# A transformer block with product-key experts and a second block with routed experts: new order of the opening, products on constants, eight expert slots, projection ahead of the norm

## The chip, the cores and the metric

The kernel is one program on 1 core of one Trainium2 chip. The metric is the device time of one execution in microseconds (us), here the median of the runs shown. Engines: TensorE (PE; its weight loads are listed as PEld), VectorE (DVE), ScalarE (ACT), GpSimd (POOL), and SyncE (SP), which only issues transfers here.

## What is computed

All arithmetic is float32, on 256 tokens of 1024 features. The kernel works on transposed activations: features on the 128 partitions, K = 8 chunks of features, T = 256 tokens along the free dimension (TT = 2 groups of 128).

```python
# first block
mod = silu(c) @ w_mod + b_mod                       # six vectors; the same for c_ctx
h  = rms_norm(x) * (1 + sc1) + sh1                  # and hc from ctx
u  = h @ w_in                                       # queries, keys/values, conv input, gates
x  = x + g1 * merge(attention, conformer_conv, gates) @ w_out
h2 = rms_norm(x) * (1 + sc2) + sh2
x  = x + g2 * peer_ffn(h2)                          # 128 x 128 product-key experts, top 16, 8 heads
x  = rms_norm(x, final_g)
# second block
h  = rms_norm(x, ln1_g_2);  proj = h @ w_in_2       # q, k, v, then the other columns
x  = x + (sigmoid(gate) * branches) @ w_out_2       # stick-breaking attention, gated linear scan
t  = rms_norm(x, ln2_g_2)
group = argmax(t @ w_rg + b_rg); two best of the 4 experts of that group
x  = x + sum over the experts chosen: combine * (silu(t @ w_gate) * (t @ w_up)) @ w_down
return rms_norm(x, final_g_2)
```

## The kernel before, in words

There is one instruction stream per engine, written by hand, with semaphores between them. `tile_plan` numbers every PSUM tile in the order in which TensorE fills it, with the engine that reads it; tile n uses bank n % 4 of `psD`, and TensorE waits until the reader of tile n - 4 has freed it. `psY` holds four further banks, which `aux(i)` gives out. The weights come in blocks of 2 MB (128 partitions x 4096 float32) through a ring of three slots (`load`, L410); SP issues block n only when TensorE has begun with the last products on block n - 3 (`w_used`).

A float32 product stands in the trace as two MATMUL instructions, an fp32r product as one. Where fp32r is used (the first block's experts), a float32 operand is split into a rounded part and the rest (hi and lo), and both are multiplied.

**Opening (L1063 to L1103, L1496 to L1509).** ACT's queue issues cT, cst, vec, xT, ctxT and conv_w, while SP issues the first w_mod blocks. TensorE: two `modulation` blocks (L558), the sum of squares of x (`stat`, L522), `modulation_sums`, the sum of squares of ctx, two more `modulation` blocks, their sums; then the projection `u0` (pairs of 128-column groups on w_in, L522), which needs the normed hT from DVE (L1509). POOL makes the normed context (L1418, L1422) from the second root on.

**w_pq.** After the first residual, `stat_x("x1")` (L544), then DVE's inverse (L1486, L1488), ACT's root and DVE's norm (L1641, L1644), then `pair` on w_pq.

**Start of the second block (L829 to L845, L1825 to L1851).** The result of the first block's experts is turned back (L832), DVE adds it to x in eight steps (L1830), `stat_x("x2")` follows, DVE scales x by final_g and the root (`normed(7)`, L1636), `stat_x("xb")` follows on that, and `normed(8)` gives hT. Only then TensorE projects q and k (`qks`, four pairs on w_in_2), which ACT copies out.

**Routed experts.** `stat_x("x3")`, the norm, the router product (L522, 128x20), eight-chunk transposes of h into token rows (`hrow`, L953), a chain of small DVE operations (L1981 to L2065) with two exponentials on ACT, the `place` products on the mask, and then seats: each expert has 64 seats per round, `hot` says which token sits where. The 16 experts are worked in pairs. One turn of the loop does one pair, in this order on TensorE: `gate_up` of both experts (L977), `seat_tokens(0)` for the next pair (L522), transposes of hid (L1016), `seat_tokens(1)`, `down` of the first (L987), two transposes of the weighted `hot` (L1026), `down` of the second, and the scatter to tokens (L1035), which adds yrow x hotT to psY in float32. ACT makes the silu and copies one half of yrow and the seated rows, DVE multiplies (L2087) and copies the other half (L2090, L2094).

```python
        mslot = [ring[(STREAM["moe"] + i) % RING] for i in range(3)] + [ar(20480 + SLOT * i, SLOT) for i in range(3)]
        ...
            used = (2, 2, 4, 4, 5, 6)
            ...
            with sp.Fori(1, turns) as n:
                for j in range(6):
                    sp.wait_ge(m_used, n * 6 + (used[j] - 6))
                    expert_load(j, ...)
```

A turn needs six blocks of 2 MB (gate, up of two experts, then two down); there are six slots, and a slot is asked for again in the turn after. Three of the first six blocks are loaded when the ring is free, three after `x_ready` reaches 32 (L479).

## Time and profile before

| | |
|---|---|
| median of 3 runs | 1931.45 us (1930.93 to 1932.64) |
| profiled execution | 1933.67 us, its span 1931.8 us |
| TensorE matmul busy | 1798.2 us (93%) |
| DVE / ACT / POOL busy | 1018.2 / 615.1 / 161.3 us |
| mean granted TensorE clock | 0.967 |
| bytes | 343.45 MB, 178 GB/s over the span |

The span runs from the first to the last instruction; the execution takes 1.9 us more than it. A line of a timeline has: start in us, length in us, engine, line of the kernel, operation, what it writes and reads, its shape, the number of instructions merged into it, and in brackets the idle time of the engine before it and what ended that. In the table of stretches each engine has its busy time and number of instructions; then come the granted TensorE clock (1.00 is full speed), the busy share of the DMA engines, and GB/s.

### The profile page before, as it was taken

The page shows a single profiled execution, that of the slowest core. Times are in us where ns is not written, and L with a number is a line of the kernel's source. Part 1 is how long each engine was busy: PE and PEld are TensorE (multiplying, and loading weights), DVE is VectorE, ACT ScalarE, POOL GpSimd, SP SyncE. Part 2 cuts the span into 40 slices and gives each one's busy share as a digit, 9 for nine tenths or more (in the row PEclk, how much of TensorE's full clock was granted, in tenths as well). Part 3 has the DMA queues.
Part 4 walks back from the last instruction along what each step waited for, and adds up shares of the span by engine and source line. Part 5 has one row for each costly group of instructions (what it writes and reads, how often), then busy time and mean ns, then how long its engine had stood idle before and what let it go on. Part 6 is the DMA issues. An engine that isn't in the chain of part 4 may idle for free. (4 is left out here: it accounts for less than half of the span.)

```text
span 1931.8 us, 23571 instructions
## 1 busy us (share of the span) xinstructions
PE 1798.2 (93%) x8906; PEld 1389.8 (72%) x8906; DVE 1018.2 (53%) x2015; ACT 615.1 (32%) x875; POOL 161.3 (8%) x81
## 2 busy tenths in 40 slices
PE   4999989999998999899999999997997989799997
PEld 2877646778887998677888888886776867544443
DVE  2469755220898876777767767765025432211112
ACT  2111264101111665333454554553353120111111
POOL 1200000000001996100000000000000000000000
PEclk8999999999999999999999999999998989799999
DMA  6466321233442222455555555555331315499993
GB/s 279 177 253 236 134 87 44 93 126 128 160 178 78 88 88 103 159 194 186 180 182 193 185 185 195 180 189 199 131 131 48 127 46 211 175 399 403 419 403 141
DMA packets 33325, 343.45 MB, mean 178 GB/s; under 512 B 3952, under 2 KB 4464, under 8 KB 5104
## 3 DMA queue, kind: packets, MB, share of 16 engines
q1 hardware_dynamic: 31680, 338.70, 46.1%
q10 hardware_dynamic: 1584, 3.90, 0.5%
q8 instruction: 42, 0.69, 0.1%
q14 instruction: 19, 0.16, 0.0%
HBM read 340.49 MB, written 2.10 MB: 177 GB/s over the span
## 5 line engine op out<-in xcount | busy, mean ns | idle before, releaser
L522 PE MATMUL psD<-xh,ring 128*128 128x256 f32 x1984 | 442.1, 384 | 18.9 <-DVE arena L1949 5.3
L522 PEld LDWEIGHTS psD<-xh,ring 128*128 128x128 f32 x1984 | 379.3, 192 | 79.4 <-issue 20.7
L797 PE MATMUL psY<-ring_r,work_r 128*128 128x512 f32 x1536 | 370.5, 396 | 11.2 <-DVE ring_r L1761 11.2
L1053 ACT ACTIVATE arena<-psD 128x512 f32<-128x512 f32 (+5 forms) x211 | 146.3, 701 | 708.9 <-PE psD L522 491.9
L797 PEld LDWEIGHTS psY<-ring_r,work_r 128*128 128x128 f32 x1536 | 283.0, 190 | 80.7 <-issue 17.8
L1053 ACT ACTIVATE ring_r<-ring 128x1024 fp32r<-128x1024 f32 x196 | 200.2, 1055 | 167.6 <-PE psY L797 113.1
L783 PE MATMUL psD<-xh_r,ring_r 128*128 128x512 f32 x544 | 194.1, 397 | 0.0
L1761 DVE TENSOR_TENSOR ring_r<-ring,ring_r 128x1024 fp32r<-128x1024 f32 x128 | 160.7, 1255 | 15.1 <-ACT ring_r L1053 15.0
L522 PE MATMUL psD<-arena,ring 128*128 128x256 f32 (+1 forms) x640 | 150.5, 395 | 7.4 <-DVE arena L1964 4.1
L785 PE MATMUL psD<-xh_r,ring_r 128*128 128x256 f32 x544 | 152.6, 280 | 0.0
L522 PEld LDWEIGHTS psD<-arena,ring 128*128 128x128 f32 (+1 forms) x640 | 119.5, 189 | 37.3 <-issue 8.8
L783 PEld LDWEIGHTS psD<-xh_r,ring_r 128*128 128x128 f32 x544 | 102.2, 188 | 24.5
L977 PE MATMUL psD<-ring,arena 128*64 128x512 f32 x384 | 111.5, 594 | 0.9 <-ACT arena L1053 0.9
L785 PEld LDWEIGHTS psD<-xh_r,ring_r 128*128 128x128 f32 x544 | 102.6, 189 | 2.6
L1436 POOL TENSOR_TENSOR ring<-cst,pick 128x384 f32<-128x384 f32 x32 | 59.2, 1849 | 538.3 <-PEq L745 536.7
L1756 DVE TENSOR_TENSOR ring_r<-ring,ring_r 128x1024 fp32r<-128x1024 f32 x68 | 83.3, 1225 | 37.7 <-ACT ring_r L1053 37.7
L522 PE MATMUL psD<-arena 128*128 128x128 f32 (+4 forms) x388 | 81.4, 354 | 15.9 <-DVEq L2036 6.9
L756 PE MATMUL psY<-xh,ring 128*128 128x256 f32 x384 | 90.7, 387 | 3.0 <-DVE pick L1712 3.0
L1535 DVE SCALAR_TENSOR_TENSOR arena<-arena,pick 128x256 f32<-128x256 f32 x232 | 92.5, 480 | 0.0
L977 PEld LDWEIGHTS psD<-ring,arena 128*64 128x64 f32 x384 | 35.6, 137 | 71.1 <-issue 71.1
L756 PEld LDWEIGHTS psY<-xh,ring 128*128 128x128 f32 x384 | 72.2, 195 | 12.1 <-issue 3.2
L2087 DVE TENSOR_TENSOR arena<-arena,psD 64x512 f32<-64x512 f32 x16 | 11.0, 690 | 130.4 <-ACT arena L1053 130.4
(238 smaller groups left out, 1906.4 us busy)
## 6 DMA issues: line engine op xcount, KB each, us to landing
ring<-in_tables SPq DMA_DIRECT2D x68, 1024.0 KB, 4.8
ring<-in_experts SPq DMA_DIRECT2D x24, 2048.0 KB, 9.2
arena<-in_experts SPq DMA_DIRECT2D x24, 2048.0 KB, 14.7
ring<-in_w_in SPq DMA_DIRECT2D x20, 2048.0 KB, 8.3
ring<-in_early_v SPq DMA_DIRECT2D x30, 1024.0 KB, 4.8
ring<-in_w_mod SPq DMA_DIRECT2D x12, 2048.0 KB, 8.4
ring<-in_early_u SPq DMA_DIRECT2D x9, 2048.0 KB, 8.5
ring<-in_mid_u SPq DMA_DIRECT2D x12, 1024.0 KB, 4.8
```

What stands on the lines that cost most here:

```text
L522: last = nc.tensor.matmul(dst, a, b, start=(i == 0), stop=(i == len(pairs) - 1))
L756: last = nc.tensor.matmul(psY[:, 1024 + 512 * (m % 2) + j * T:1024 + 512 * (m % 2) + (j + 1) * T], col_slot[m % 3][:, at:at + P], hT[:, k, ...
L783: nc.tensor.matmul(bank[:, :], u_hi[c % 2][:, k * P:(k + 1) * P], xh_r[:, :, k, :], start=(k == 0), stop=(k == K - 1), skip_group_check=True)
L785: last = nc.tensor.matmul(bank[:, 0:T], lo[:, k * P:(k + 1) * P], h_hi[:, k, :], start=False, stop=(k == K - 1), skip_group_check=True)
L797: last = nc.tensor.matmul(psY[:, t * D + h * 512:t * D + (h + 1) * 512], wgt[:, b, t * P:(t + 1) * P], v[:, h * 512:(h + 1) * 512], start= ...
L977: last = nc.tensor.matmul(psD[bank][lo:lo + 64, :], lhs, wt[:, k * 512:(k + 1) * 512], start=(k == 0), stop=(k == K - 1))
L1053: return nc.scalar.activation(dst, src, f, **kw)
L1436: nc.gpsimd.tensor_tensor(one_b[:, h, DVE_B:], iota8[:, 0:8 - DVE_B], e2.broadcast_to([P, 8 - DVE_B, P]), ALU.subtract).then_inc(b_diff, 1)
L1535: s[j % 2] = mark(stt(acc, y[:, j:j + T], conv_w[:, m * TAPS + j:m * TAPS + j + 1], acc, ALU.mult, ALU.add))
L1756: tt(col_lo[unit][:, 0:D], col_slot[unit][:, 0:D], u_hi[c % 2].bitcast(F32), ALU.subtract).then_inc(u_lo_ready, 1)
L1761: tt(lo, a, v_hi[b].bitcast(F32), ALU.subtract).then_inc(v_lo_ready, 1)
L2087: tt(hid[64 * side:64 * (side + 1), :], sgl[64:128, side, :], psD[bank][64:128, :], ALU.mult).then_inc(hid_done, 1)
```

## The change

1. Opening: SP's queue issues cT, cst, xT and vec ahead of the w_mod blocks; ACT's queue keeps ctxT and conv_w. TensorE takes the sum of squares of x before the modulation, and that of ctx between blocks 2 and 3. The modulation blocks get the order shown. POOL waits for hT before it norms the context.
2. `keep(n, bank)`: n float32 products of the identity with 512 columns of constants, in a bank that nobody reads. There are 27 of them: 8 in the opening, 3 after `stat_x("x1")`, 3 after `stat_x("x3")`, 7 after the transposes of h, 6 before the first `seat_tokens`.
3. Second block: DVE makes `xg` = x * final_g * ln1_g beside the residual. The projection `qks` runs on xg, the two sums of squares (of x, and of x * final_g, squared by ACT) come after its first pair, and DVE multiplies q and k by the common root while it copies them out. hT comes from the same root.
4. Routed experts: seats and scatter use fp32r on split operands (hrow, yrow in hi and lo parts); the combine weight goes into hid instead of `hot` (a product with `seat_col`, copied to `seat_scale`). The scatter of a turn runs in the next turn, after its first `gate_up`. Four turns are written out, the loop goes over fours. `place` leaves the tile plan and uses psY.
5. Eight slots for the expert blocks, free when `gate_up` or `down` is done; the second w_out2 block goes to a place of its own in the arena, and the first expert blocks are issued from `osb_ready` on.

```diff
+            sp.dma_start(cT[:].rearrange("p a b -> p (a b)"), w["cT"]).then_inc(in_c, 16)
+            sp.dma_start(cst[:], w["cst"]).then_inc(in_small, 16)
+            sp.dma_start(xT[:].rearrange("p a b -> p (a b)"), w["xT"]).then_inc(in_x, 16)
+            sp.dma_start(vec[:], w["vec"]).then_inc(in_small, 16)
             for i in range(4):
                 load(STREAM["mod1"] + i, w["w_mod"][i])
...
-            act.dma_start(cT[:].rearrange("p a b -> p (a b)"), w["cT"]).then_inc(in_c, 16)
-            act.dma_start(cst[:], w["cst"]).then_inc(in_small, 16)
-            act.dma_start(vec[:], w["vec"]).then_inc(in_small, 16)
-            act.dma_start(xT[:].rearrange("p a b -> p (a b)"), w["xT"]).then_inc(in_x, 16)
...
+            def keep(n, bank):
+                for _ in range(n):
+                    nc.tensor.matmul(bank, ident, cst[:, 0:512], start=True, stop=True)
+
+            pe.wait_ge(in_small, 32)
+            keep(2, psD[3])
+            pe.wait_ge(sq_ready, 1)
+            stat("x", ones, chunks(sq))
             pe.wait_ge(c_silu, 1)
             pe.wait_ge(mparts_zero, 1)
             for b in range(2):
                 modulation(b, STREAM["mod1"] + b, b)
-            pe.wait_ge(in_small, 32)
-            pe.wait_ge(sq_ready, 1)
-            stat("x", ones, chunks(sq))
             modulation_sums(TILE["mod1_"], 0)
+            keep(2, psD[3])
+            modulation(2, STREAM["mod1"] + 2, 1)
             pe.wait_ge(sq_ready, 2)
             stat("ctx", ones, chunks(csq))
-            for b in range(2, 4):
-                modulation(b, STREAM["mod1"] + b, 1)
+            keep(2, psD[3])
+            modulation(3, STREAM["mod1"] + 3, 1)
             modulation_sums(TILE["mod1_"] + 1, 2)
+            keep(2, psD[3])
...
             pool.wait_ge(rstd_ready, 2)
+            pool.wait_ge(h_ready, K)
...
             stat_x("x1", sq, 0)
+            keep(3, aux(2))
...
-            stat_x("x2", sq2, 1)
-            stat_x("xb", sq2, 2)
             for m in range(4):
                 wt = use(STREAM["w_in2"] + m // 2)
-                pair(TILE["qks"] + m, wt, 2 * (m % 2), hT, 1 if m == 2 else 0, None if m else (h_part, K))
+                pe.wait_ge(xg_ready, 2)
+                pair(TILE["qks"] + m, wt, 2 * (m % 2), xg, 1 if m == 2 else 0, None if m else (xg_ready, 0))
+                if m == 0:
+                    stat_x("x2", sq2, 1)
+                    stat_x("xb", sq2g, 2)
...
+            r = rstd(8)
+            for k in range(K):
+                stt(hT[:, k, :], xT[:, k, :], both_g[:, k:k + 1], r, ALU.mult, ALU.mult).then_inc(h_part, 1)
+            for m in range(4):
+                ps = take(TILE["qks"] + m).rearrange("p (a t) -> p a t", a=2)
+                dst = (qs if m < 2 else ks)[:, 2 * (m % 2):2 * (m % 2) + 2, :]
+                stt(dst, ps, SBD ** -0.5 if m < 2 else 1.0, over(r, 2), ALU.mult, ALU.mult).then_inc(tile_free["dve"], 1)
...
-            stat_x("x3", sq2, 3, frees=1)
+            stat_x("x3", sq2, 3)
+            keep(3, aux(3))
...
+            keep(7, aux(3))
             pe.wait_ge(mask_ready, 1)
...
+            def turn(it, t, after):
+                def slot(j):
+                    b = 6 * t + j
+                    pe.wait_ge(m_loaded[b % 8], it * 48 + (16 * (b // 8) + 16))
+                    return mslot[b % 8]
+
+                pe.wait_ge(seated_ready, it * 8 + (2 * t + 2))
+                if after:
+                    pe.wait_ge(yrow_ready, it * 16 + (4 * t - 2))
+                gate_up(1, 0, slot(0), slot(1))
+                if after:
+                    pe.wait_ge(yrow_ready, it * 16 + 4 * t)
+                    scatter()
+                turn_seats()
+                gate_up(3, 1, slot(2), slot(3))
+                pe.wait_ge(hot_ready, it * 4 + (t + 2))
+                pe.wait_ge(hotT_ready, it * 4 + (t + 1))
+                seat_tokens(0)
+                pe.wait_ge(hid_done, it * 8 + (2 * t + 2))
+                for f in range(4):
+                    last = nc.tensor.transpose(psD[2][:, f * P:(f + 1) * P], hid[:, f * P:(f + 1) * P], ident)
+                last.then_inc(hidT_done, 1)
+                pe.wait_ge(seated_ready, it * 8 + (2 * t + 3))
+                seat_tokens(1)
+                pe.wait_ge(hidT_ready, it * 4 + (t + 1))
+                down(1, 0, slot(4))
+                down(3, 1, slot(5))
+
+            pe.wait_ge(hrow_ready, 4)
+            keep(6, psD[1])
             pe.wait_ge(rounds_ready, 1)
...
+            def scatter():
+                for m in range(K):
+                    for rows in (yrow_hi, yrow_lo):
+                        last = nc.tensor.matmul(psY[:, m * T:(m + 1) * T], rows[:, m * P:(m + 1) * P], hotT,
+                                                start=False, stop=False, skip_group_check=True)
+                last.then_inc(scattered, 1)
...
+            def slot_free(b, it=0):
+                n, j = divmod(b - 8, 6)
+                done = gu_done if j < 4 else down_done
+                sp.wait_ge(done, it * 8 + (2 * n + (1 if j in (0, 1, 4) else 2)))
...
+            for n in range(4):
+                ps = psD[(TILE["hrow"] + n) % 4]
+                dve.wait_ge(hrow_hi_ready, n + 1)
+                at = slice((n % 2) * 512, (n % 2 + 1) * 512)
+                tt(hrow_lo[:, n // 2, at], ps, hrow_hi[:, n // 2, at].bitcast(F32), ALU.subtract).then_inc(hrow_ready, 1)
             dve.wait_ge(rexp, 2)
```

## Rows read from the trace of the kernel before

**Rows 1.** Page, part 1: busy time of TensorE over the span

```profile
PE 1798.2 (93%) x8906; PEld 1389.8 (72%) x8906; DVE 1018.2 (53%) x2015; ACT 615.1 (32%) x875; POOL 161.3 (8%) x81
```

**Rows 2.** Stretches: busy PE, PEld, DVE, ACT, POOL, then clock, DMA share, GB/s

```profile
9.50:29.00 19.50, 6.01 (x32) 0.74 (x32) 0.00 (x0) 2.25 (x3) 0.00 (x0) 0.66 0.98 413
44.00:49.50 5.50, 1.46 (x14) 1.37 (x13) 4.08 (x6) 0.43 (x2) 4.98 (x2) 0.73 1.00 429
...
419.00:424.00 5.00, 4.83 (x12) 3.87 (x13) 4.24 (x14) 0.00 (x0) 0.00 (x0) 0.50 0.54 170
...
1335.70:1341.60 5.90, 5.87 (x16) 4.49 (x16) 1.12 (x3) 2.90 (x4) 0.00 (x0) 0.62 0.99 418
...
1637.80:1644.40 6.60, 6.54 (x31) 6.57 (x32) 2.69 (x7) 0.00 (x0) 0.00 (x0) 0.50 1.02 434
...
1662.00:1666.90 4.90, 3.75 (x16) 3.49 (x16) 0.58 (x2) 0.59 (x1) 0.00 (x0) 0.50 0.00 0
...
1733.06:1763.78 30.72, 29.58 (x151) 13.90 (x151) 4.05 (x7) 5.32 (x8) 0.00 (x0) 1.00 0.97 405
```

**Rows 3.** DMA issues: KB, us to landing (x; first w_in_2 block, issued 1323.3)

```profile
xh<-in_xT ACTq DMA_DIRECT2D x1, 1024.0 KB, 25.2
...
ring<-in_w_in SPq DMA_DIRECT2D x1, 2048.0 KB, 8.0
```

**Rows 4.** Timeline of the opening

```profile
29.42 5.37 PE L522 MATMUL psY<-arena,cst 128*128 128x256 f32 x16 [11.79 <-ACT arena L1053]
...
42.81 5.96 POOL L1418 TENSOR_TENSOR arena<-arena,work 128x2048 f32<-128x2048 f32 x1 [42.36 <-ACT work L1053]
...
45.78 3.04 DVE L1503 TENSOR_TENSOR mod<-mod,vec 128x32 f32<-128x32 f32 x1 [1.35 <-ACT mod L1053]
...
49.30 4.77 POOL L1422 TENSOR_SCALAR arena<-arena,gx,mod 128x256 f32<-128x256 f32 x8 [0.52 <-DVE gx L1506]
...
49.70 15.84 PE L522 MATMUL psD<-xh,ring 128*128 128x256 f32 x64 [4.24 <-DVE xh L1509]
```

**Rows 5.** Timeline, first products on w_pq

```profile
419.17 20.99 PE L522 MATMUL psD<-xh,ring 128*128 128x256 f32 x82 [4.09 <-DVE xh L1644]
```

**Rows 6.** Timeline, start of the second block

```profile
1325.38 3.23 DVE L1830 SCALAR_TENSOR_TENSOR xh<-psD,mod,xh 128x256 f32<-128x256 f32 x8 [0.82 <-PE psD L832]
...
1345.02 27.86 PE L522 MATMUL psD<-xh,ring 128*128 128x256 f32 x128 [3.42 <-DVE xh L1636]
```

**Rows 7.** Timeline from the router to the first turn

```profile
1637.86 6.99 PE L522 MATMUL psD<-arena,xh 128*128 128x20 f32 x32 [3.36 <-DVE xh L1636]
...
1650.15 0.16 DVE L2010 TENSOR_REDUCE arena<-arena 128x2 f32<-128x8 f32 x1 [3.58 <-ACT arena L1053]
...
1659.65 0.42 DVE L2074 TENSOR_TENSOR arena<-cst,arena 128x256 f32<-128x256 f32 x1
...
1662.52 3.75 PE L522 MATMUL psD<-arena 128*128 128x128 f32 x16 [5.43 <-DVE psY L2075]
...
1671.61 7.48 PE L977 MATMUL psD<-ring,arena 128*64 128x512 f32 x33 [0.88 <-ACT arena L1053]
```

**Rows 8.** Timeline, one turn of the expert loop

```profile
1733.06 7.51 PE L977 MATMUL psD<-ring,arena 128*64 128x512 f32 x33
...
1760.16 3.69 PE L1035 MATMUL psY<-arena 128*128 128x256 f32 x16 [0.89 <-DVE arena L2094]
```

**Rows 9.** Timeline, rows that serve as prices

```profile
34.63 1.84 PE L522 MATMUL psD<-cst,arena 128*128 128x2 f32 x16
...
1303.62 0.28 PE L785 MATMUL psD<-xh_r,ring_r 128*128 128x256 f32 x1
1303.73 0.40 PE L783 MATMUL psD<-xh_r,ring_r 128*128 128x512 f32 x1
...
1423.43 7.13 PE L522 MATMUL psD<-ring,xh 128*128 128x512 f32 x16
...
1583.01 0.69 DVE L1612 TENSOR_TENSOR arena<-psD,arena 128x512 f32<-128x512 f32 x1 [3.66 <-PE psD L522]
```

More of the change, by code:

```diff
@@ L495, in _ @@
+            fours = sp.value_load(rounds[0:1, 1:2], min_val=PAIRS // 4, max_val=PAIRS // 4 * ROUNDS)
+            with sp.Fori(1, fours) as it:
+                for b in range(24):
+                    slot_free(b, it)
+                    expert_load(b, w["experts"][bass.ds(it % (PAIRS // 4) * 24 + b, 1)].rearrange("a p n -> (a p) n"))
             for half in range(2):
@@ L967, in seat_tokens, with gate_up @@
                     last = group(psD[0][:, j * P:(j + 1) * P],
-                                 [(hrow[:, t, k * P:(k + 1) * P], hot[:, t, :]) for t in range(TT)])
+                                 [(rows[:, t, k * P:(k + 1) * P], hot[:, t, :])
+                                  for t in range(TT) for rows in (hrow_hi, hrow_lo)])
                 last.then_inc(seated_done, 1)
-            def gate_up(bank, side, wg, wu, frees):
+            def gate_up(bank, side, wg, wu):
                 for k in range(K):
@@ L2095, in _ @@
+            dve.wait_ge(yrow_ready, turns * 4)
+            dve.sem_inc(yrow_all, 1)
             dve.wait_ge(scattered, turns)
```

275 lines of the change are left out of this document (145 added, 130 removed).

## The prediction

> **What bounds the kernel now.** I read the page first, then the list of what TensorE waited for, then the table of stretches with the granted clock, and last the timelines of the places that the change touches. TensorE is busy 93% of the span [rows 1], so a gain can only come from its idle gaps, from stretches at the lower clock, or from products taken off it. The change touches five places, and each has one of these. In the opening TensorE waits 11.79 us for the square of x [rows 4], and x had landed only 25.2 us after its issue [rows 3], while the w_mod blocks filled the DMA engines at 413 GB/s [rows 2]. Around each norm it idles 3 to 5 us and then works for some us at clock 0.50, the lower of its two levels (1.2 GHz): on w_pq, on the second sum of squares, on the router and on the first seats [rows 2]. In the expert loop a turn takes 30.72 us at clock 1.00 [rows 2], the eight turns fill 1671.61 [rows 7] to 1917.4, and no row shows TensorE waiting for a load; but the DMA engines are at 0.97 and 405 GB/s there, and the highest rate elsewhere is 429 to 434 [rows 2], so the loop is near both bounds.
>
> **Opening.** All bytes ahead of x in its queue are now cT and cst (0.33 MB); beside it runs ctxT (1.05 MB) from the other queue. 0.33 + 1.05 + 1.05 = 2.4 MB at 430 GB/s are 5.7 us, from a start at about 2.2 us: x lands near 8.5 us instead of 27.4, vec near 9, the three first w_mod blocks (4.9 us each) near 13.7, 18.6 and 23.4. Then, with my estimates between the prices of the rows (a sum of squares is 3.6 us at full clock and 5.4 as it ran here [rows 4]; a group of sums 1.84 [rows 9]): two constant products and the sum of x to 18; modulation 0 and 1 to 22 (block 3 is issued at about 19 and lands at 28.3); copies and sums to 24.5, constants to 26, modulation 2 to 28 (its first product issues w_in, which lands near 33 behind block 3), the sum for ctx to 32, constants, modulation 3 to 35.5, copy and sums to 38. Before, DVE's small addition to mod took 3.04 us, exactly until POOL's 5.96 us operation was over [rows 4]; POOL now waits for hT, so it takes 0.2. hT starts near 39 and TensorE near 39.8 instead of 49.70. The 64 products took 15.84 us, partly at the lower clock; full clock is 64 x 0.217 = 13.9 (27.86 / 128 = 0.217 [rows 6]), 1.5 less counting what the ramp leaves. POOL's context (5.96 + 4.77 us [rows 4]) starts at about 42 and ends at 53, just as these products end. What follows is bound by TensorE as before, so this is a clean shift: **-11.4 us**. Bounds: -7, if all of it runs at the lower clock and the constants are not covered; -14, if full clock holds from the start.
>
> **w_pq.** A constant product is two instructions of 512 columns, 2 x 0.43 = 0.86 us (16 took 7.13 [rows 9]); three are 2.6 us inside a gap of 4.09 [rows 5], so they cost nothing; their cover is DVE's and ACT's norm, without it they would cost 2.6. The first 5.0 us after the gap ran at 0.50 [rows 2], so up to half of it comes back: **-2.6 us**. Bounds 0 (clock falls all the same) and -2.8.
>
> **Second block.** DVE's residual takes 3.23 us for eight steps [rows 6]; xg adds a step of some 0.25 us to each, all done by about 1331. The first products could start at 1327, but what is late next is w_in_2: its first block, issued at 1323.3, lands 8.0 us later [rows 3], at 1331.3. From there: one pair 6.95 (27.86 / 4 [rows 6]), two sums 7.2, three pairs 20.9, and 2.5 us for a cold start, since TensorE idles 4.7 us before and there is no constant product here; the same idle time before the second sum gave 5.87 us for 16 instructions at mean clock 0.62 [rows 2]. End at 1368.9, before 1345.02 + 27.86 = 1372.9. **-4.0 us**; bounds -6.5 (no cold start) and -1 (ACT's eight extra squares or DVE late). DVE's root is ready near 1352 and hT near 1355, ahead of the next user of hT at 1369. DVE's later norm of x (3.3 us) and its four copies of q and k (0.69 each [rows 9]) run beside 14 us of products on v.
>
> **Router to first turn.** The three constants (2.6 us) fill a gap of 3.36 [rows 7]. The router's 32 instructions took 6.99 us at 0.50; at full clock 16 of them follow DVE's norm and the others take 0.115 each (1.84 / 16 [rows 9]), the logits come 2.1 us earlier. DVE's 3.58 us wait before 1650.15 is for an exponential behind ACT's copies of hrow [rows 7]; copies and table load move with the transposes, so that end comes 2.8 us earlier. Seven constants take 6.0 us, from about 1644.5 to 1650.5, the mask is due at 1651.9. DVE's four subtractions for hrow_lo cost 4 x 0.69 = 2.8 us [rows 9] and stand on its path, with 0.4 for two small additions and 0.3 back from the place products. So hot is ready about when it was, 1660.1. TensorE began its seats at 1662.52, held by the clearing of psY [rows 7], which the first scatter now waits for instead. Six constants from 1654.9 end at 1660.0, just in time; with the register load I take 1661.0: -1.5. The seats: 2 x 3.75 us at 0.50 [rows 2, 7] become 2 x 1.85: -3.8. **-5.3 us**; bounds 0 and -8.
>
> Here one price is open: an fp32r product of 128 columns with new weights. Products of 256 columns follow each other in 0.11 us (1303.62 to 1303.73), and 16 float32 instructions with only two columns still take 1.84 us, 0.115 each [rows 9]. I take 0.115 for 128 columns too, since that row is the one in which the load of 128x128 weights decides; then splitting in hi and lo leaves a seat group as long as it was (16 instructions, 1.8 us). The other end is 0.058, half of the 256-column row. The Trainium skill, TensorE: Matmul & The Clock Gate, section LDWEIGHTS (loading the stationary operand), speaks against a gain from this part: it puts a weight load at columns divided by 1.2 GHz whatever else is streamed, 107 ns for 128. By that page's figure, as an estimate, a seat group would be 1.7 us, by the column count 0.9; the two-column row agrees with the page.
>
> **Loop.** Per turn: the scatter was 3.62 us (16 float32 instructions, from 1760.16 to the next gate_up, one turn of 30.72 after 1733.06 [rows 8]), now 16 fp32r at 0.115: -1.8. Its wait of 0.89 us for DVE [rows 8] goes, as the next gate_up stands ahead of it: -0.9. Four small products of two instructions each, with 64-column weights, at most 8 x 0.115: I take +0.5. Seats 0. So 28.5 us; bounds 27.3 (seats at the other price; the first seat group must still cover ACT's silu and DVE's product) and 29.8. DVE's four subtractions and ACT's four copies per turn (2.8 and 2.4 us) run beside `down` and `gate_up`; their cover is 20 us. Loads: six blocks of 2.1 MB in 28.5 us would be 441 GB/s, above 434. But eight are there before the first turn, so 40 are left, the first issued 7 us into turn 0 and the last needed 24 us into turn 7: 217 us for 84 MB, 387 GB/s. At 405 GB/s they take 207 us. So the slots bridge it, and loads don't bind by 10 us. Eight turns are 228 us. The last scatter waits for two ACT copies and a subtraction, 2.2 us instead of 0.9. 230.2 us against 245.9: **-15.7 us**, bounds -26 and -6.
>
> **Sum.** 11.4 + 2.6 + 4.0 + 5.3 + 15.7 = 39.0 us. The profiled execution took 1933.67 us, so 1894.7 on its scale; the median of the runs is 2.2 us below, so **1892.5 us**. A measurement of this kernel tells about 0.2% (3.9 us) from no change.
>
> **Rivals.**
> *The constants don't hold the clock.* For: they come after gaps, and the stretch 9.5 to 29 had 0.66 with 6 us of products in it [rows 2]. Against: the constants leave 1.5 us of the 4.09 on w_pq, and the loop, with gaps of 0.9 us in it, stands at 1.00 [rows 2, 8]. If they don't, each constant costs 1.72 us. Opening -6; w_pq 5.2 us into a gap of 4.1: +1.1; second block -4; three constants overrun by 1.8, seven end near 1661.5 instead of the mask at 1654.8, six more 10.3 us, seats at the old price: first turn near 1683, +11.5; loop -15.7. About -13: **1918 us**. Chance 0.09.
> *Loads bind in the loop.* For: 0.97 busy at 405 GB/s already [rows 2]. It decides below 387 GB/s. If the rate is 370, 40 loads take 227 us, and the loop lasts 7 + 227 + 3.6 for the last `down` + 4.1 to the end of the scatter = 242 us, a gain of 4 instead of 15.7: **1904 us**. Chance 0.09.
> *The opening is bound by w_in and w_mod, not by x.* Before w_in can be used, 12.4 MB must land, and w_in is only issued when block 2 is in use. If interleaving with ctx holds w_mod back by one block (5 us), the gain there is 6: **1898 us**. Chance 0.08.
> *The other side: loads one at a time.* SP now waits for each slot in order; if each load begins only when the one before has landed, it costs 8.0 us [rows 3], and 40 take 320 us: the loop lasts some 335 us, +89, less the 23.3 elsewhere: **1997 us**. It decides from 30.7 + 23.3 / 8 = 33.6 us per turn, 374 GB/s from start to end. Against: before, SP waited in the same way and reached 405. Chance 0.03.
> *The change does less than it says*, as the fours are rounded up and idle turns are run: no, before there were eight turns, which is two fours. Not priced.
>
> **Numbers.** My forecast, all five parts within their bounds, has 0.71. Its own range is 1880 to 1905: the bounds of the parts don't all fall on one side. The upper end goes to 1910 to take in the two rivals at 1898 and 1904 with their own spread; left out are the first rival, the last, and a part of the low end. Faster by over 0.2%: 0.95; within 0.2%: 0.01; slower: 0.04.
>
> **What the profile after would show.** x lands within 10 us; u0 starts at 38 to 42 with clock 1.00; DVE's addition to mod takes 0.2 us. The first products on w_pq, the router and the seats stand at clock 1.00. The first pair of the second block starts at 1320 (1331.3 less the shifts so far), released by the load of w_in_2. Turns 28.5 us apart, no wait for a load; a seat group of 1.8 us. The forecast is wrong if a load releases gate_up or down, if TensorE's constants are the last thing ahead of w_pq or of the first seats, or if turns stay above 30 us.

## The result, and the profile after

The changed kernel takes **1898.64 us** (median of 4 runs, 1895.24 to 1900.81), the kernel before beside it 1931.36 us (1930.93 to 1932.64): ratio 0.9828, 95% interval 0.9811 to 0.9845. The profiled execution took 1899.66 us, with a span of 1897.6, against 1933.67 and 1931.8. The forecast of 1892.5 was 6.1 us too low, and the measured time lies inside its range of 1880 to 1910; the profiled executions are 34.0 us apart, not 39.0.

First the page of the kernel after, part 1, for TensorE [rows 1], then its table of stretches, columns as in [rows 2]:

```profile
PE 1806.9 (95%) x9024; PEld 1404.1 (74%) x9024; DVE 1031.9 (54%) x2060; ACT 623.3 (33%) x891; POOL 159.4 (8%) x81
```

```profile
251.90:256.90 5.00, 4.97 (x12) 2.86 (x13) 2.60 (x8) 2.67 (x8) 0.00 (x0) 0.50 0.73 246
407.40:412.40 5.00, 5.00 (x17) 2.79 (x18) 4.05 (x13) 0.00 (x0) 0.00 (x0) 1.00 0.71 229
1317.80:1327.60 9.80, 9.80 (x33) 8.21 (x34) 0.00 (x0) 4.00 (x8) 0.00 (x0) 0.72 0.98 418
1638.20:1643.00 4.80, 4.76 (x11) 2.20 (x12) 4.00 (x29) 0.00 (x0) 0.00 (x0) 1.00 0.86 355
...
1646.00:1648.20 2.20, 2.12 (x16) 2.12 (x16) 0.00 (x0) 0.03 (x1) 0.00 (x0) 0.84 0.00 0
1649.10:1658.70 9.60, 9.53 (x32) 2.74 (x32) 0.00 (x0) 1.30 (x2) 0.00 (x0) 0.73 0.00 0
1700.00:1728.30 28.30, 28.07 (x162) 15.23 (x160) 5.36 (x10) 6.52 (x11) 0.00 (x0) 1.00 1.00 426
...
1883.10:1888.50 5.40, 5.32 (x16) 4.14 (x16) 1.22 (x4) 3.10 (x4) 0.00 (x0) 0.69 0.00 0
```

TensorE is at full clock on w_pq, where it was at 0.50 [rows 2], and in the constants ahead of the seats. Its clock falls again in places that the forecast had at full clock: the second seat group (1646), the first `gate_up` behind it (1649.1, 9.6 us for what takes 7.0 in later turns) and the last sum of squares (1883.1). The turn is 28.3 us instead of 30.72. Below, "cold" means at the lower clock.

Timeline of the opening, after; it answers to [rows 4]:

```profile
9.55 1.91 ACT L1122 ACTIVATE arena<-xh 128x2048 f32<-128x2048 f32 x1 [4.76 <-DMA xh<-in_xT]
9.75 3.78 PE L620 MATMUL psD<-cst 128*128 128x512 f32 x4 [9.75 <-DMA vec<-in_vec]
...
13.32 4.92 PE L554 MATMUL psY<-arena,cst 128*128 128x256 f32 x16
...
37.03 0.19 DVE L1567 TENSOR_TENSOR mod<-mod,vec 128x32 f32<-128x32 f32 x1 [3.37 <-ACT mod L1122]
...
38.44 13.98 PE L554 MATMUL psD<-xh,ring 128*128 128x256 f32 x64
...
40.36 4.51 POOL L1481 TENSOR_TENSOR arena<-arena,work 128x2048 f32<-128x2048 f32 x1 [39.91 <-DVE xh L1573]
```

x is there at 9.5 instead of 27.4, DVE's addition takes 0.19 instead of 3.04 us, and the 64 products of u0 take 13.98 instead of 15.84 and begin 11.3 earlier. The first four constant instructions take about 0.9 us each, twice the 0.43 of later ones, so they are cold, although the granted clock of 9.70 to 13.30 reads 1.00: at the start of this kernel the lengths show the lower clock and that column doesn't.

Timeline of the later places, after; they answer to [rows 5], [rows 6] and [rows 7]; the last three rows are the end of the loop:

```profile
407.38 5.00 PE L554 MATMUL psD<-xh,ring 128*128 128x256 f32 x16 [1.51 <-DVE xh L1708]
...
1317.80 9.84 PE L554 MATMUL psD<-arena,ring 128*128 128x256 f32 x32 [4.76 <-DMA ring<-in_w_in]
...
1619.69 5.60 PE L554 MATMUL psD<-arena,xh 128*128 128x20 f32 x32 [0.79 <-DVE xh L1700]
...
1638.24 5.42 PE L620 MATMUL psD<-cst 128*128 128x512 f32 x12 [1.36 <-DVE hrow_lo L2131]
...
1878.59 0.39 PE L1056 MATMUL psY<-hotT,yrow_hi 128*128 128x256 f32 x1 [2.19 <-DVEq L2190]
...
1881.58 2.74 DVE L2193 TENSOR_TENSOR xh<-psY,xh 128x256 f32<-128x256 f32 x8 [3.10 <-PE psY L1056]
...
1883.14 5.32 PE L576 MATMUL psY<-arena,cst 128*128 128x256 f32 x16 [1.60 <-ACT arena L1122]
```

The same events in both traces give the account of the gain:

| part | event | before | after | gain | forecast |
|---|---|---|---|---|---|
| opening | end of u0's 64 products | 65.37 | 52.25 | 13.1 | 11.4 |
| (nothing changed) | attention, at L698 (before L657) | 292.39 | 280.60 | -1.3 | 0 |
| w_pq | first tile copied out | 429.41 | 415.87 | 1.75 | 2.6 |
| second block | first products on v | 1372.72 | 1355.11 | 4.1 | 4.0 |
| its middle | sum of squares x3 | 1630.88 | 1612.71 | 0.6 | 0 |
| router to first turn | first `gate_up` | 1671.61 | 1649.17 | 4.3 | 5.3 |
| loop, last scatter | DVE's last addition begins | 1917.50 | 1881.58 | 13.5 | 15.7 |
| last sum and norm | last norm begins | 1925.54 | 1891.27 | -1.7 | 0 |

Together 34.3 us. Where the gain fell short, TensorE's clock was low in most rows; so the experiments ask two things, what each part is worth by itself, and what the clock follows.

### The profile page after: what moved, and what is told of

Same layout as the page of the kernel before. It is cut to its first block and busy times, and to the rows that moved or that the text cites. A ratio compares the mean times of both kernels' runs of the same rounds, so it can differ in the third digit from the quotient of the medians.

```text
span 1897.6 us, 23793 instructions
## 1 busy us (share of the span) xinstructions
PE 1806.9 (95%) x9024; PEld 1404.1 (74%) x9024; DVE 1031.9 (54%) x2060; ACT 623.3 (33%) x891; POOL 159.4 (8%) x81
## 5 line engine op out<-in xcount | busy, mean ns | idle before, releaser
L554 PE MATMUL psD<-xh,ring 128*128 128x256 f32 x1856 | 411.0, 382 | 8.9 <-DVE arena L2037 5.6
L554 PEld LDWEIGHTS psD<-xh,ring 128*128 128x128 f32 x1856 | 351.5, 191 | 67.0 <-issue 15.4
L1122 ACT ACTIVATE arena<-psD 128x512 f32<-128x512 f32 (+4 forms) x187 | 132.2, 715 | 616.1 <-PE psD L554 473.2
L554 PE MATMUL psD<-arena,ring 128*128 128x256 f32 x704 | 167.6, 398 | 12.2 <-DMA ring<-in_w_in 4.8
L554 PEld LDWEIGHTS psD<-arena,ring 128*128 128x128 f32 x704 | 133.6, 192 | 44.7 <-issue 8.8
L1028 PE MATMUL psD<-arena 128*64 128x512 f32 x320 | 115.8, 602 | 0.7 <-ACT arena L1122 0.7
L1028 PE MATMUL psD<-ring,arena 128*64 128x512 f32 x192 | 87.2, 608 | 0.0
L1503 POOL TENSOR_TENSOR work<-work,pick 128x1024 f32<-128x1024 f32 x32 | 79.1, 2473 | 0.0
```

The costliest lines, as they stand in the source:

```text
L554: last = nc.tensor.matmul(dst, a, b, start=(i == 0), stop=(i == len(pairs) - 1))
L1028: last = nc.tensor.matmul(psD[bank][lo:lo + 64, :], lhs, wt[:, k * 512:(k + 1) * 512], start=(k == 0), stop=(k == K - 1))
L1122: return nc.scalar.activation(dst, src, f, **kw)
L1503: nc.gpsimd.tensor_tensor(one_a[:, h], one_a[:, h], g.broadcast_to([P, 8, P]), ALU.mult).then_inc(a_ready, 1)
```

## The experiments

Each median stands beside 1898.64 us for the changed kernel. Runs of one and the same kernel lie up to 8 us apart here, so where a difference is small, the traces decide and not the medians.

**No constants.** `keep` does nothing:

```diff
-                for _ in range(n):
-                    nc.tensor.matmul(bank, ident, cst[:, 0:512], start=True, stop=True)
+                return
```

> The changed kernel with all 26 constant products left out (eight in the opening, three ahead of w_pq, three ahead of the router, twelve ahead of the first seats). Theory (they hold the clock where TensorE would idle): w_pq starts where it did but at the lower clock for about 5 us, +1.8; the router at the lower clock, logits 2 us later; both seat groups at the lower clock, 3.7 us each, so the first gate_up comes 2 to 4 us later than now. In the opening about 9 us of constants leave TensorE's path, but sums and modulations then run partly at the lower clock: between -4 and +2. Together +1 to +8, 1900 to 1907 us. Rival (the clock falls or stays whatever they do, as it fell in the second seat group right behind six of them): the time falls by what they occupy, the opening by 4 us or more and nothing elsewhere, 1891 to 1895 us.

(There are 27 constants, not 26.) Measured: 1902.11 us (1897.32 to 1905.57), +3.5, inside the theory's 1900 to 1907; the ratio 0.9843 [0.982, 0.9867] overlaps that of the changed kernel. The timeline without constants, opening and router:

```profile
37.78 15.74 PE L554 MATMUL psD<-xh,ring 128*128 128x256 f32 x64 [1.32 <-DVE xh L1572]
...
1621.87 6.86 PE L554 MATMUL psD<-arena,xh 128*128 128x20 f32 x32 [3.37 <-DVE xh L1699]
```

u0 starts 0.7 us earlier, but at the lower clock, and ends 1.1 later. The router takes 6.86 instead of 5.60, and from the sum x3 to the first seats it is 31.5 instead of 30.4. The two seat groups up to the first `gate_up` take 8.7 us instead of 6.1. On w_pq the first tile is copied out 17.9 us after the sum x1 begins, instead of 16.2. So the constants hold the clock for the most part and are worth 6.5 us in these four places (1.1 + 1.7 + 1.1 + 2.6); the profiled executions are 5.7 apart. The opening's eight give only 1.1: there they cost TensorE nearly as much as they save.

**Scatter ahead of `gate_up`.** The order of the turn undone, the hi and lo products kept:

```diff
                 if after:
-                    pe.wait_ge(yrow_ready, it * 16 + (4 * t - 2))
-                gate_up(1, 0, slot(0), slot(1))
-                if after:
                     pe.wait_ge(yrow_ready, it * 16 + 4 * t)
                     scatter()
+                gate_up(1, 0, slot(0), slot(1))
```

> The changed kernel with each turn's scatter ahead of the next turn's first gate_up, waiting for both hi and lo rows, instead of behind it. Theory (the order hides the copy and subtraction behind a gate_up): the last scatter shows this wait, 2.19 us, so each of the seven other turns gets about 2.2 us longer, 30.5 instead of 28.3, and if the wait lets the clock fall as at the end of the kernel, up to 2 us more: +15 to +25, 1914 to 1924 us. Rival (the loads set the turn, and the order is worth nothing, the gain being that of eight slots): turns stay at 28.3 to 28.8, 1899 to 1903 us.

Measured: 1915.76 us (1912.87 to 1917.11), +17.1, as the theory said. The first row of the scatter in its timeline, and one turn in its table of stretches:

```profile
1709.19 0.36 PE L1056 MATMUL psY<-hotT,yrow_hi 128*128 128x256 f32 x1 [2.23 <-DVE yrow_lo L2185]
```

```profile
1700.00:1730.87 30.87, 28.42 (x160) 15.16 (x162) 5.36 (x10) 6.51 (x11) 0.00 (x0) 1.00 0.98 408
```

The wait is 2.23 us; before, with one copy instead of a copy and a subtraction, it was 0.89 [rows 8]. The turn is 30.87 us, no shorter than the 30.72 of before: **in the old order the split into hi and lo saves nothing**, since the longer way to yrow_lo takes back what the cheaper products give. Only with the scatter behind the next `gate_up` does it pay. The clock stayed at 1.00 in spite of the wait.

**Scatter in float32,** on the hi rows alone, order as changed:

```diff
-                    for rows in (yrow_hi, yrow_lo):
-                        last = nc.tensor.matmul(psY[...], rows[:, m * P:(m + 1) * P], hotT, ...)
+                    last = nc.tensor.matmul(psY[...], yrow_hi[:, m * P:(m + 1) * P].bitcast(F32), hotT.bitcast(F32), ...)
```

> The changed kernel with the scatter as eight float32 matrix products on the hi rows alone (the lo rows are still made but left out of the product, so the output lacks their part), instead of sixteen fp32r ones. Theory (a float32 product of 256 columns costs 2 x 0.217 us, an fp32r one 0.115): the scatter goes from 1.9 to 3.6 us, turns from 28.3 to 30.0, +13 to +15 in eight scatters, 1912 to 1915 us. Rival (the turn has slack behind loads or behind DVE and the shorter scatter bought little): under +5, 1904 us at most.

Measured: 1910.28 us (1908.72 to 1911.89), +11.6, a little under the 13 to 15 expected; its turn is 29.86 us, 1.56 longer, and its scatter:

```profile
1712.33 3.72 PE L1055 MATMUL psY<-hotT,yrow_hi 128*128 128x256 f32 x16
```

Eight scatters at 1.56 are 12.5. With the 0.89 of the wait this is the turn's whole gain: 30.72 - 1.56 - 0.89 = 28.27, measured 28.30. So the cheaper scatter gives 1.6 us and not the 1.8 of the forecast, and the rest of the turn, with the four small products that it put at +0.5, costs next to nothing.

**Six blocks back.** `slot_free` waits as if there were six slots:

```diff
-                n, j = divmod(b - 8, 6)
+                n, j = divmod(b - 6, 6)
```

> The changed kernel with its eight slots, but each load waits until the block six places back, not eight, has been used, which is what six slots would do. Theory (loads don't bind with eight, by some 10 us, and nearly do with six; a turn of six loads at 425 GB/s takes 29.6 us): TensorE waits for a load in each turn, the turn goes from 28.3 to 29.6 to 30.5 us, +8 to +18, 1907 to 1917 us. Rival (the loads were never near, TensorE's own work alone set the turn): no wait, 1899 us as now.

Measured: 1895.80 us (1893.81 to 1898.65), no slower; the theory expected a wait for a load in each turn, and the rival was right. One turn:

```profile
1700.00:1728.30 28.30, 28.07 (x160) 15.23 (x158) 5.36 (x10) 6.51 (x10) 0.00 (x0) 1.00 1.01 428
```

The turn is 28.30 to the hundredth, at 428 GB/s. At that rate six blocks take 29.4 us, 1.1 more than a turn, so each turn eats into the lead; but eight blocks are still loaded ahead of the first turn here, and, as an estimate, eight turns lose 8 x 1.1 = 9 us of it, the time of two blocks. A kernel that also starts with six was not tried.

This run shows something else. Up to the loop it is the changed kernel, instruction for instruction, and it reached the first silu at 1653.06, the changed kernel at 1658.85. Of these 5.8 us, 2.0 lie ahead of the attention (1.7 of them in one sum of 16 products, 3.72 us here and 5.41 in the changed kernel), 2.6 in the attention's first 28 us, 1.2 between w_pq and the end of the first block's experts. The attention's start in it, against 251.90 above:

```profile
249.90:254.90 5.00, 4.74 (x22) 2.95 (x23) 3.90 (x12) 3.88 (x11) 0.00 (x0) 1.00 0.75 249
```

From the attention's first product behind its wait of 2.22 us (251.93 in the changed kernel) to the one behind its next wait (0.87 us, 280.60) all kernels run the same products. The traces show three lengths: 26.0 us (this and `scatter_first`), 27.3 (before, `no_constants`, `scatter_f32`, `seats_f32`, `sums_first`, `ctx_late`) and 28.6 to 28.7 (the changed kernel, `no_pool_wait`, `x_first_alone`, `more_constants`). The clock falls behind that wait or it doesn't, and comes back sooner or later, from run to run. **That is the -1.3 of the table, in a part that nobody changed**, and, at up to 2.7 us, a good part of the spread between runs.

**More constants,** in five places: ahead of w_pq, of the second block's first pair, behind each of the two seat groups ahead of the loop, and on both sides of the last scatter:

```diff
-            keep(3, aux(2))
+            keep(4, aux(2))
...
+            keep(4, aux(3))
...
             seat_tokens(0)
+            keep(1, psD[1])
             pe.wait_ge(seated_ready, 1)
             seat_tokens(1)
+            keep(1, psD[1])
...
+            keep(2, psD[2])
             pe.wait_ge(yrow_all, 1)
             scatter()
+            keep(2, psD[2])
             stat_x("x4", sq2, 4)
```

> The changed kernel with constants in five more places: a fourth ahead of w_pq, four ahead of the second block's first pair (a wait of 4.8 us for w_in_2), one behind each of the two seat groups ahead of the loop, two ahead of the last scatter (2.2 us wait) and two behind it. Theory (the shortfall against the forecast is the lower clock in these places, and products that fill the wait hold it up): first pair of the second block 7.0 instead of 9.8 us, second seat group at 0.11 a product and first gate_up of turn 0 in 7.0 instead of 9.7 us at the price of up to 0.9, last scatter at 0.12 a product and the last sum of squares in 3.6 instead of 5.3. Together -5 to -9, 1890 to 1894 us. Rival (the clock doesn't follow what is put into a gap of a few us; it fell in the second seat group behind six constants): under 2 us, or up to 2 slower, 1897 to 1901 us.

Measured: 1893.24 us (1887.08 to 1894.51), -5.4. Its stretches (both seat groups, the first `gate_up`, the last scatter and sum), then its first pair:

```profile
1645.90:1647.80 1.90, 1.90 (x18) 1.88 (x17) 0.00 (x0) 0.00 (x0) 0.00 (x0) 1.00 0.00 0
1648.70:1655.70 7.00, 7.00 (x33) 2.21 (x32) 0.00 (x0) 1.16 (x1) 0.00 (x0) 1.00 0.00 0
...
1875.60:1877.60 2.00, 1.96 (x16) 1.97 (x17) 0.00 (x0) 0.00 (x0) 0.00 (x0) 1.00 0.00 0
1879.40:1883.10 3.70, 3.70 (x17) 2.94 (x16) 1.19 (x4) 3.07 (x4) 0.00 (x0) 1.00 0.00 0
```

```profile
1317.43 7.17 PE L554 MATMUL psD<-arena,ring 128*128 128x256 f32 x32 [1.40 <-DMA ring<-in_w_in]
```

Each place is at full clock and as long as the theory said: 7.0 instead of 9.7 for the first `gate_up`, 3.7 instead of 5.3 for the last sum, 7.2 instead of 9.8 for the first pair. The trace gives 2.7 in the pair, 2.8 from seats to silu and 2.4 at the end, 7.9 in all; the median and the profiled executions show 5.4 and 5.5. The difference lies between the sum x3 and the first seats, which took 32.9 us instead of 30.4, where this edit changed nothing:

```profile
1636.38 7.11 PE L620 MATMUL psD<-cst 128*128 128x512 f32 x12 [1.35 <-DVE hrow_lo L2135]
```

The same six constants that took 5.42 us in the changed kernel began cold here (0.74 over the group), took 7.11 and ran 2.0 us past `hot`, which was ready at 1640.94. So a constant costs its length once the clock is low under it, and what is held in one place can partly be lost in the next.

**Seats in float32,** on the hi rows alone:

```diff
-                                 [(rows[:, t, k * P:(k + 1) * P], hot[:, t, :])
-                                  for t in range(TT) for rows in (hrow_hi, hrow_lo)])
+                                 [(hrow_hi[:, t, k * P:(k + 1) * P].bitcast(F32), hot[:, t, :].bitcast(F32))
+                                  for t in range(TT)])
```

> The changed kernel with each seat group as 8 float32 products of 128 columns on the hi rows alone (the lo rows are made but left out of it, so the output lacks their part) instead of 16 fp32r ones. Theory of the prediction (a product of 128 columns is set by its weight load, 0.115 us an instruction in either form): a seat group stays 1.8 us at full clock, turns stay at 28.3: within 2 us of 1899. Rival (the columns decide for fp32r and it was the cheaper form): a turn longer by 1 us or more, 1907 us and up. In the same run: does the clock fall in the second seat group ahead of the loop, as with fp32r? Then it is the shape, not the form.

Measured: 1891.51 us (1890.25 to 1893.57), -7.1, outside both ranges. One turn is 28.41 us and not 28.30, so the theory's price was right: 16 instructions of 128 columns take as long in either form, 0.11 to 0.12 us each. The Trainium skill, TensorE: Matmul & The Clock Gate, section LDWEIGHTS (loading the stationary operand), puts a weight load at its columns divided by 1.2 GHz, as an estimate 107 ns for 128 columns; the trace agrees, with these 0.11 to 0.12 us. The gain is elsewhere, first in its second seat group and first `gate_up`:

```profile
1644.60:1646.70 2.10, 2.05 (x16) 1.86 (x16) 0.00 (x0) 0.00 (x0) 0.00 (x0) 1.00 0.00 0
1647.30:1654.30 7.00, 6.95 (x32) 2.21 (x32) 0.00 (x0) 1.28 (x1) 0.00 (x0) 1.00 0.00 0
```

They are at full clock, with gaps of 0.69 us around them as in the changed kernel. In the eight traces with fp32r seats and no constant between the groups, the first silu came 9.4 to 9.8 us after the first `gate_up` began; here it came after 7.1. The kernel before supports the same reading: its float32 seat groups were themselves cold (0.50), and `gate_up` behind them began at 1.00, its silu 7.1 us later [rows 7], while behind the cold fp32r groups of `no_constants` it came after 9.5. So at this place it is the form, not the shape, that goes with the fall; why is not shown.

From seats to silu that is 3.3 us. Another 2.4 lie at the end, where the last scatter, in fp32r and behind the same wait of 2.19 us, stayed at 1.00 and so did the last sum:

```profile
1878.82 3.69 PE L576 MATMUL psY<-arena,cst 128*128 128x256 f32 x16 [1.60 <-ACT arena L1122]
```

With 1.3 in the attention and 0.9 lost in eight turns that makes 6.1, as far as the profiled executions are apart.

**x first, alone:** the kernel before, its four transfers moved from ACT's queue to SP's, in the order of the change, and nothing else.

```diff
-            act.dma_start(xT[:].rearrange("p a b -> p (a b)"), w["xT"]).then_inc(in_x, 16)
...
+            sp.dma_start(xT[:].rearrange("p a b -> p (a b)"), w["xT"]).then_inc(in_x, 16)
+            sp.dma_start(vec[:], w["vec"]).then_inc(in_small, 16)
             for i in range(4):
                 load(STREAM["mod1"] + i, w["w_mod"][i])
```

> The kernel before with one edit: cT, cst, x and vec issued on SyncE's queue ahead of w_mod, as the change does; TensorE's order, no constants and the second processor's context operation as before. Theory (the late x was only half of it: TensorE waited 11.8 us for it, but then w_mod and DVE's 3.0 us addition beside GpSimd stand next): x lands by 10 us, u0 starts near 42 instead of 49.7, so -6 to -9, 1921 to 1925 us. Rival (moving x alone gives the whole opening, the reordering and constants nothing): -11 to -13, 1917 to 1920 us.

Measured: 1924.03 us (median of 6, 1919.70 to 1927.38), ratio 0.9964 [0.9947, 0.9981], -6.4. Its timeline:

```profile
36.05 3.05 DVE L1503 TENSOR_TENSOR mod<-mod,vec 128x32 f32<-128x32 f32 x1 [1.35 <-ACT mod L1057]
...
39.97 15.49 PE L526 MATMUL psD<-xh,ring 128*128 128x256 f32 x64 [4.24 <-DVE xh L1509]
```

u0 starts at 39.97 instead of 49.70, so the queue gives 9.7 of the opening's 11.3; the addition beside POOL is still 3.05 us, and the products still run at the lower clock. With 0.35 from their shorter time it is 10.1 by the end of these products, of 13.1. The median shows -6.4, inside the theory's range, and the profiled executions are 10.1 apart; so this part's worth lies between, and the rival (-11 to -13) is not borne out.

**No wait on GpSimd:**

```diff
             pool.wait_ge(rstd_ready, 2)
-            pool.wait_ge(h_ready, K)
```

> The changed kernel without GpSimd's wait for hT: its context operation may run as soon as the root is there, near 34, beside DVE's work on hT. Theory (the two share something, and GpSimd's operation stalled DVE's addition to mod for 3.0 us before): DVE's addition takes 3 us instead of 0.19, its steps for hT 0.5 instead of 0.33 each, u0 starts 3 us later, +3, 1901 to 1903 us. Rival (the addition was held by something else, or GpSimd is through before it matters): u0 at 38.4, 1899 us.

Measured: 1896.59 us (1895.57 to 1902.94), not told from 1898.64. Its timeline:

```profile
34.11 4.51 POOL L1480 TENSOR_TENSOR arena<-arena,work 128x2048 f32<-128x2048 f32 x1 [33.66 <-ACT work L1122]
...
36.95 1.72 DVE L1566 TENSOR_TENSOR mod<-mod,vec 128x32 f32<-128x32 f32 x1 [3.37 <-ACT mod L1122]
...
38.98 3.98 DVE L1572 TENSOR_SCALAR xh<-arena,gx,mod 128x256 f32<-128x256 f32 x8
39.14 4.78 POOL L1484 TENSOR_SCALAR arena<-arena,gx,mod 128x256 f32<-128x256 f32 x8 [0.52 <-DVE gx L1569]
```

DVE's addition, 0.19 us by itself, lasts until POOL's operation is over: 34.11 + 4.51 = 38.62, 36.95 + 1.72 = 38.67. The eight steps beside POOL's next ones take 3.98 instead of 2.67. u0 starts 1.1 us later and ends 1.7 later. So the stall is real, but POOL's early start leaves only its tail; the theory's 3 us was too much. The Trainium skill, SBUF — State Buffer, section "SBUF: two separate sides", says that VectorE and GpSimd share one port pair, and that when a VectorE operation with two inputs in SBUF meets a GpSimd operation that reads SBUF, the one that starts first holds the pair for its whole instruction; the two end times agree.

**Sums first,** in the second block:

```diff
+            stat_x("x2", sq2, 1)
+            stat_x("xb", sq2g, 2)
             for m in range(4):
...
-                if m == 0:
-                    stat_x("x2", sq2, 1)
-                    stat_x("xb", sq2g, 2)
```

> The changed kernel with the two sums of squares ahead of the four unscaled pairs of the second block, not behind the first of them. Theory (the gain there comes from the projection not waiting for a norm at all; the sums then fill TensorE's wait for w_in_2, but run at the lower clock behind a gap of their own): the pairs end within 2 us of now, -2 to +2, 1897 to 1901 us. Rival (the order is what gains: a pair under the squares of ScalarE): +4 or more, 1903 us and up.

Measured: 1891.17 us (1889.31 to 1895.92), -7.5, better than either expected. Its timeline:

```profile
1309.14 1.97 PE L874 MATMUL psD<-cst,arena 128*128 128x128 f32 x16 [1.38 <-DVE arena L1888]
1311.62 2.35 PE L576 MATMUL psY<-arena,cst 128*128 128x256 f32 x8 [0.51 <-ACT arena L1121]
1314.15 1.13 PE L576 MATMUL psY<-arena,cst 128*128 128x256 f32 x4 [0.18 <-ACT arena L1121]
1315.46 4.58 PE L576 MATMUL psY<-arena,cst 128*128 128x256 f32 x20 [0.18 <-ACT arena L1121]
1319.88 27.79 PE L554 MATMUL psD<-arena,ring 128*128 128x256 f32 x128
```

The sums do useful work in the wait for w_in_2, and their gaps are 0.51 us at most, so the clock never fell; the load was there when they ended. From the end of the transposes the pairs end 36.4 us later, 42.1 in the changed kernel: -5.7. I had taken a sum as 7 us *behind* a wait; it fits *into* it.

**ctx late:**

```diff
-            sp.dma_start(vec[:], w["vec"]).then_inc(in_small, 16)
+            load(STREAM["mod1"], w["w_mod"][0])
+            load(STREAM["mod1"] + 1, w["w_mod"][1])
+            sp.dma_start(ctxT.rearrange("p a t -> p (a t)"), w["ctxT"]).then_inc(in_ctx, 16)
+            sp.dma_start(vec[:], w["vec"]).then_inc(in_vec, 16)
...
-            pe.wait_ge(in_small, 32)
+            pe.wait_ge(in_small, 16)
...
-            dve.wait_ge(in_small, 32)
+            dve.wait_ge(in_small, 16)
+            dve.wait_ge(in_vec, 16)
```

> The changed kernel with the opening's transfers in another order: ctx on SyncE's queue behind the second w_mod block, vec behind it with a semaphore of its own, and TensorE's first constants waiting for cst alone. Theory (the opening is a chain on TensorE that begins with vec, at 9.75 us, and x, at 9.5; ctx is not needed before 27): x lands near 6, the sum for x starts near 9 instead of 13.3, u0 near 35 instead of 38.4: -2 to -4, 1895 to 1897 us. Rival (the opening is bound by the bytes of w_mod and w_in, the DMA engines being full to 30 us): u0 stays at 38, 1899 us.

Measured: 1900.46 us (1899.07 to 1902.02), +1.8: neither. Its timeline:

```profile
21.58 0.43 DVE L1552 TENSOR_SCALAR work<-psY 128x256 f32<-128x256 f32 x1 [19.63 <-DMA vec<-in_vec]
```

x landed at 9.03 instead of 9.55, so ctx was only 0.5 us of its delay. The w_mod blocks issued behind x in the same queue are the likely rest; no run held them back. And the late vec held DVE to 21.58, ACT's root behind it, and ACT's copy of the second modulation behind that. u0 started at 43.38.

**Together:** the edits of `sums_first` and `more_constants` (without the four ahead of the pair), and

```diff
+            keep(2, aux(2))
             pe.wait_ge(conv_ready, K)
             stat("mean", ones, chunks(convz))
...
+            keep(2, aux(2))
             for n in range(8):
                 ps = tile(TILE["v"] + n)
...
+            keep(2, aux(2))
             pe.wait_ge(q_ready, 8)
```

> The changed kernel with the sums of the second block first (as in sums_first), the constants of more_constants except those ahead of the second block's first pair, which the sums now fill, and two constants in each of three waits of 1.9 to 2.2 us that the changed kernel still has (ahead of the sum for the mean, ahead of the products for v, ahead of the attention). Theory (each place adds up on its own): -5.8 in the second block, -5.2 at seats, last scatter and last sum (as measured in more_constants), and up to 2.6 where the clock fell in the attention's start in some runs and not in others: 1885 to 1889 us, and a narrower spread between runs. Rival (the clock's dips only move: what is held in one place falls in the next): no better than either edit alone, 1891 to 1894 us.

Measured: 1885.95 us (median of 5, 1884.27 to 1887.88), as the theory said, with a narrow spread. The constants ahead of the attention missed: the 2.22 us wait comes after its first products, not before them, and is unchanged; that stretch took 27.2 us. Here too the six constants ahead of the seats began cold and took 7.11 us.

**Together, with another opening:** vec stays where it was in the queue, on `in_vec`, and

```diff
-            pe.wait_ge(in_small, 32)
-            keep(2, psD[3])
+            pe.wait_ge(in_small, 16)
+            keep(5, psD[3])
...
             modulation_sums(TILE["mod1_"], 0)
-            keep(2, psD[3])
+            keep(1, psD[3])
             modulation(2, STREAM["mod1"] + 2, 1)
             pe.wait_ge(sq_ready, 2)
             stat("ctx", ones, chunks(csq))
-            keep(2, psD[3])
             modulation(3, STREAM["mod1"] + 3, 1)
```

> The same, with the opening changed again: vec on a semaphore of its own, TensorE's first five constants waiting for cst alone, one constant fewer behind the first modulation sums and none ahead of the last w_mod block. Theory (the opening is TensorE's chain, in which 3.9 us of constants stand with no gap under them, while w_in lands at about 34.5): u0 starts at 35.5 to 36.5 instead of 38.4 with the clock held, -2 to -3 against the kernel called together. Rival (w_mod's landing bounds it, or the clock falls without them as it did when all were gone): u0 at 37.8 or its products at 15.7 us, 0 to +1 against it.

Measured: **1884.06 us** (median of 5, 1882.89 to 1885.17), ratio 0.9757 [0.9743, 0.977], against 0.9764 [0.975, 0.9777] for `together`; 14.6 us below the changed kernel. Its opening:

```profile
6.91 7.06 PE L621 MATMUL psD<-cst 128*128 128x512 f32 x10 [6.91 <-DMA cst<-in_cst]
...
13.81 3.62 PE L555 MATMUL psY<-arena,cst 128*128 128x256 f32 x16
...
30.63 1.90 PE L591 MATMUL psY<-ring,cS 128*2 128x512 f32 x16 [0.73 <-DMA ring<-in_w_mod]
...
36.06 13.98 PE L555 MATMUL psD<-xh,ring 128*128 128x256 f32 x64
```

u0 at 36.06 instead of 38.32, -2.3; the medians are 1.9 apart, with overlapping intervals. Five constants overran x's square (ready at 11.4) by 2.4 us, yet the sum ran at full clock (3.62 instead of 4.92) and was over at 17.4 instead of 18.2, and TensorE then waits for w_mod (0.73 us ahead of the last block), which now decides.

## Why the prediction was right, and by how much it missed

**Opening, -11.4: right in its chain; it gave 13.1.** x landed at 9.5 (8.5 forecast), u0 started at 38.44 (39.8), the 64 products took 13.98 (13.9). DVE's addition took 0.19, as said. What was not seen: vec, which shares a semaphore with cst, released TensorE's first constants at 9.75, and these, cold, delayed the sum by 1.9 us.

**w_pq, -2.6: it gave 1.75.** The clock was full, but the step took all of a cold stretch as lost. The first 16 products take 5.00 us at full clock, since they follow DVE's norm piece by piece; 16 at 0.217 would be 3.5.

**Second block, -4.0: right to 0.1,** cold start included, with w_in_2 as the releaser at 1317.80. (The 1320 of the prediction is a slip: 1331.3 less its own 11.4 and 2.6 is 1317.3.) `sums_first` shows that a simple exchange would have given 5.7 more, and `more_constants` 2.7.

**Router to first turn, -5.3: it gave 4.3.** The step that failed is "2 x 3.75 us become 2 x 1.85": the price was right (0.11 a product), the clock under it was not. The six constants held it through the first group only. The logits came 1.4 and not 2.1 earlier, for the router's own products ran at 0.86; the transposes behind them ran at 0.50, so DVE's wait for the exponential ended 1.0 us earlier and not 2.8. The chain of waits was right: the mask and `hot` came just as the constants ended; for the first seven that was in part luck, since they and the mask both came later than forecast.

**Loop, -15.7: it gave 13.5.** The turn is 28.30 (28.5 forecast), 1.6 us better over eight. Against it stand 2.7 for the cold first `gate_up`, which the forecast didn't have, and 1.1 for the last scatter at a clock of 0.68. "Loads don't bind" held, with more to spare than the eight slots suggest.

**Behind the loop, 0: it cost 1.7,** the sum x4 at the lower clock behind gaps of 2.2 and 1.6 us. I had costed nothing there. In `scatter_first` and `seats_f32` the same scatter and sum stayed at full clock, so this loss varies between kernels that don't differ there. And 1.3 us were lost in the attention, by no act of the change.

The rivals: constants that don't hold the clock were wrong as a whole, but in the seats half right. Loads that bind and a bound by w_in didn't come. The central error, w_pq apart, is one: I charged the lower clock only where [rows 2] showed it, and took every place with a new wait or new kind of product at 1.00. That the total came within 6 us is in part luck: the opening's 1.7 us over the forecast made up for part of the shortfall.

## What to carry to other kernels

Where an engine waits for a load, look first for real work of the same block to put there; constants are the second choice, and they belong into the gap itself, between small products too, and not ahead of a run of them. Leave room behind them, for cold constants take up to twice as long and can run past what they wait for, as they did in `more_constants`. Price a cheaper product together with the wait that its extra operand makes: here the split paid only because the scatter was moved behind the next `gate_up`. When runs of one kernel lie several us apart, compare the stretches that the edit doesn't touch before crediting a few us to the edit.

## What the runs showed of the hardware that was not expected

- A group of 16 fp32r products and one of 16 float32 instructions, of the same shape and nearly the same length (1.8 to 1.9 and 2.05 us), with the same 0.69 us gaps, left the clock differently: at 0.84 and then 0.73 with fp32r, at 1.00 with float32 (one run; eight with fp32r show the slow `gate_up`). With one constant behind each fp32r group both the second group and the `gate_up` were at 1.00 too.
- At the end of the kernel the form does not decide alone. Behind the same wait of 2.19 us, the same 16 fp32r products took 2.9 to 3.2 us in six traces and 2.2 us in two (`scatter_first`, `seats_f32`); the last sum behind them took 5.2 to 6.8 us in the six and 3.69 in the two. The float32 scatter took 5.41 us and the sum behind it 3.69.
- Behind a wait of 2.22 us the same products, at the same place of the program, ran at 0.50 in one run and at 1.00 in another.
- A DVE operation of 0.19 us lasted 1.72 or 3.04 us, to within 0.05 us of the end of GpSimd's.
